# Gate one-hots made on POOL, and more gathered rows worked off in the u loop of a PEER layer

## The reference, cut to what matters

```python
def peer_ffn(h, w_query, sub_keys, u_tab, v_tab):
    q = (h @ w_query).reshape(bsz, seq, 8, 2, 128)
    scores = einsum('blhcd,hckd->blhck', q, sub_keys)      # 128 keys per half
    s_top, i_top = top_k(scores, 16)
    cand_s = s_top[..., 0, :, None] + s_top[..., 1, None, :]      # 16 x 16 pairs
    best_s, pos = top_k(cand_s, 16)
    expert_idx = i_top[0] * 128 + i_top[1]                 # at pos: one of 16384
    gates = softmax(best_s)
    act = gelu(einsum('td,thkd->thk', h_blk, u_tab[expert_idx]))
    out = einsum('thkd,thk->td', v_tab[expert_idx], gates * act)
```

## Time and profile before

| | |
|---|---|
| median of three runs | 3818.42 us |
| profiled execution, its own time | 3818.46 us |
| its span | 3816.6 us |
| busy: PE, DVE, ACT, POOL | 3387.5, 2730.8, 1932.5, 607.7 us |
| expert stage, a block | 36.3 us |
| u loop | from 2544 to 3233 us of the span |
| v loop | from 3233 to 3808 us |

### The profile page before, as it was taken

The page is one execution under the profiler, slowest core; times in us unless marked ns, Lnnn a source line. Parts: engine busy times, 40 slices in busy tenths (PEclk is TensorE's granted clock), DMA queues, the critical chain, the costliest instruction groups (busy, mean ns, idle before and its releaser), DMA issues. The chain is left out here.

```text
span 3816.6 us, 46791 instructions
## 1 busy us (share of the span) xinstructions
PE 3387.5 (89%) x16253; PEld 2821.9 (74%) x16253; DVE 2730.8 (72%) x3557; ACT 1932.5 (51%) x2328; POOL 607.7 (16%) x428
## 2 busy tenths in 40 slices
PE   7697745999999999999299977799999987999998
PEld 3485544777777777777188856589999987777776
DVE  8316536999999999999544226337888766788887
ACT  1225414777777777777124334225878874332332
POOL 0000011001011011010200000000000254555652
PEclk9898867999999999999589978899999998999999
DMA  7520107999999999999633301134545689999997
GB/s 296 176 67 2 46 30 260 375 379 374 378 375 374 378 375 373 379 374 363 239 97 92 98 22 45 63 139 160 183 177 216 258 331 363 358 371 379 385 381 274
DMA packets 217467, 954.88 MB, mean 250 GB/s; under 512 B 23344, under 2 KB 85040, under 8 KB 142448
## 3 DMA queue, kind: packets, MB, share of 16 engines
q1 hardware_dynamic: 161872, 734.91, 52.0%
q0 software_dynamic: 46816, 167.80, 11.7%
q10 hardware_dynamic: 8640, 50.34, 3.2%
HBM read 864.92 MB, written 88.05 MB: 250 GB/s over the span
## 5 line engine op out<-in xcount | busy, mean ns | idle before, releaser
L1394 DVE TENSOR_TENSOR w_low<-w_raw,w_high 128x2048 fp32r<-128x2048 f32 x399 | 908.6, 2288 | 91.3 <-ACT w_high L1323 86.4
L1323 ACT ACTIVATE w_high<-w_raw 128x2048 fp32r<-128x2048 f32 x399 | 765.0, 1917 | 329.9 <-PE ps L125 182.3
L123 PE MATMUL ps<-w_high,xT_high 128*128 128x512 f32 x1056 | 433.6, 411 | 21.8 <-issue 21.8
L2462 DVE TENSOR_TENSOR uv_lo<-uv_raw,uv_hi 128x2048 fp32r<-128x2048 f32 x128 | 293.3, 2292 | 198.8 <-ACT uv_hi L2267 198.0
L124 PE MATMUL ps<-w_low,xT_high 128*128 128x512 f32 x1056 | 418.4, 396 | 0.0
L125 PE MATMUL ps<-w_high,xT_low 128*128 128x512 f32 x1056 | 418.1, 396 | 0.0
L123 PE MATMUL ps<-h4T_high,uv_hi 128*128 128x384 f32 x1024 | 355.9, 348 | 18.5 <-ACT a_out L2304 14.9
L123 PE MATMUL ps<-uv_hi,w_hi 128*128 128x512 f32 x768 | 306.3, 399 | 45.7 <-DVE w_lo L2477 34.8
L124 PE MATMUL ps<-h4T_low,uv_hi 128*128 128x384 f32 x1024 | 346.5, 338 | 0.0
L125 PE MATMUL ps<-h4T_high,uv_lo 128*128 128x384 f32 x1024 | 346.4, 338 | 0.0
L2267 ACT ACTIVATE uv_hi<-uv_raw 128x2048 fp32r<-128x2048 f32 x128 | 244.7, 1912 | 149.0 <-PE ps L125 119.2
(11 more groups left out here) (515 smaller groups left out, 6991.0 us busy)
## 6 DMA issues: line engine op xcount, KB each, us to landing
w_raw<-in_w_gate_up SPq DMA_DIRECT2D x267, 1024.0 KB, 6.9
w_raw<-in_w_down SPq DMA_DIRECT2D x132, 1024.0 KB, 6.9
uv_raw<-in_peer_u SPq DMA_DIRECT2D x64, 1024.0 KB, 5.3
uv_raw<-in_peer_v SPq DMA_DIRECT2D x64, 1024.0 KB, 9.3
wbuf_ada<-in_w_ada SPq DMA_DIRECT2D x12, 2048.0 KB, 8.8
a_rows<-a_out SPq DMA_DIRECT2D x128, 192.0 KB, 2.0
g_rows<-spread ACTq DMA_DIRECT2D x12, 2048.0 KB, 8.4
qT<-g_rows SPq DMA_DIRECT2D x16, 1536.0 KB, 15.1
```

The lines of the kernel that those rows point to most:

```text
L123: pe.matmul(out, l_hi, r_hi, start=first, stop=False)
L1323: act.activation(w_hi[:, n % SPLIT, :], w_raw[:, n % RAW, :], ACT.Copy).then_inc(s_wh, 1)
L1394: dve.tensor_tensor(w_lo[:, n % SPLIT, :], w_raw[:, n % RAW, :], w_hi[:, n % SPLIT, :].bitcast(F32), ALU.subtract).then_inc(s_wl, 1)
L2462: dve.tensor_tensor(uv_lo[:, n % 2, :], uv_raw[:, n % 2, :], uv_hi[:, n % 2, :].bitcast(F32), ALU.subtract).then_inc(s_lo, 1)
```

## The change

- Both hots of every token are made on POOL, one instruction each: tensor_scalar with is_equal against the index, and for first_hot a multiplication with the gate in the same instruction. That is 8 instructions a round, 768 in all. POOL's program becomes a walk over the plan: in each step the hots, then the gathers that the plan lets go in this step (`gather_step`).
- `gated_hots` on ACT and `one_hots` on DVE go. selT keeps three parts of five, for the negated copies are not needed; PE waits for one semaphore in place of two.
- ORDER is (1, 0, 2, 3) and SPARSE 1: tile 0 is selected second, in steps 12 to 22 rather than 24 to 34. Rows start in step 24: one a step to 33, mostly two to 45, six in 46 to 59, four to 63, two a step in the v loop. 137 of the 256 are then done in the u loop.
- The rounds go 1, 1, 2, ... in steps 11 to 33 and 2, 3, 2, ... in steps 34 to 59. MIDDLE_AT (from which row on four more homes are used) goes from 8 to 43, LATE_AT (the tenth home) from 84 to 140.
- In the expert stage a tile room_xT of 432 floats a partition, which nothing uses, is allocated ahead of xT_high.

```diff
     xe = sb(stage, "xe", [P, D])
+    sb(stage, "room_xT", [P, 432])
     xT_hi, xT_lo = (sb(stage, f"xT_{x}", [P, 2, 4 * P], F32R) for x in ("high", "low"))
...
-    ORDER, SPARSE = (1, 2, 0, 3), 2
+    ORDER, SPARSE = (1, 0, 2, 3), 1
-    selT = sb(peer, "selT", [P, 2, 5, P])
+    selT = sb(peer, "selT", [P, 2, 3, P])
-    MIDDLE_AT, LATE_AT = 8, 84
+    MIDDLE_AT, LATE_AT = 43, 140
-    hots_in = [[1] + [2] * 15 + [1], [2, 2, 2, 1] * 4 + [2, 2], [2, 3] * 6 + [2]]
-    hots_from = (11, 28, 46)
-    rows_in = {45: 2, 46: 4} | {n: 4 for n in range(47, NG)} | {NG + k: 3 if k % 9 else 2 for k in range(NG - 1)}
+    hots_in = [[1, 1, 2] * 4 + [1, 1, 1, 2] * 2 + [2, 2, 2], [2, 3] * 6 + [2], [2, 3] * 6 + [2]]
+    hots_from = (11, 34, 47)
+    rows_in = {n: 1 for n in range(24, 34)} | {n: 2 for n in range(34, 47)} | {n: 6 for n in range(47, 60)} | {n: 4 for n in range(60, NG)}
+    rows_in |= {34: 5, 46: 6}
+    rows_in |= {NG + k: 2 if k % 3 == 0 else 2 for k in range(NG - 1)}
...
+            def hots(r):
+                s, tile = r % HOTS, 4 * r // P
+                if r * 4 % P == 0:
+                    pool.wait_ge(s_selh, tile + 1)
+                if r >= HOTS:
+                    pool.wait_ge(s_gb, r - HOTS + 1)
+                at = 4 * r % P
+                for q in range(4):
+                    pool.tensor_scalar(first_hot[:, s, q, :], iota_row[:, :], selT[:, tile % 2, 0, at + q:at + q + 1],
+                                       selT[:, tile % 2, 2, at + q:at + q + 1], ALU.is_equal, ALU.mult).then_inc(s_hotp, 1)
+                    pool.tensor_scalar(second_hot[:, s, q, :], iota_row[:, :], selT[:, tile % 2, 1, at + q:at + q + 1], None,
+                                       ALU.is_equal).then_inc(s_hotp, 1)
...
+            for n in range(2 * NG):
+                for kind, x, c in plan[n]:
+                    if kind == "H":
+                        for k in range(c):
+                            hots(x + k)
+                for g in gathers_at[n]:
+                    gather(g)
...
             def gate_products(r):
-                pe.wait_ge(s_hot, 2 * (r + 1))
-                pe.wait_ge(s_hota, 3 * (r + 1))
+                pe.wait_ge(s_hotp, 8 * (r + 1))
```

More of the change, by code:

```diff
@@ L2058, in emit @@
         sem(f"peer_{x}") for x in ("scores", "scores_read", "shifted", "exp", "selected", "sel_turned", "sel_here"))
-    s_hi, s_lo, s_used, s_pa, s_gelu, s_hot, s_dist, s_hota, s_gb, s_gt2, s_gst = (
-        sem(f"peer_{x}") for x in ("high", "low", "split_used", "dots", "gelu", "one_hots", "distances", "gated_hots", "gate_products",
+    s_hi, s_lo, s_used, s_pa, s_gelu, s_hotp, s_gb, s_gt2, s_gst = (
+        sem(f"peer_{x}") for x in ("high", "low", "split_used", "dots", "gelu", "one_hots", "gate_products",
                                    "gates_spread", "gates_stored"))
@@ L2083, in emit @@
     UNITS_T, UNIT_EXP = 21, 14
-    turns_at = {x: [at + k for k in range(11)] for x, at in enumerate((0, 12, 24, 35))}
-    hots_in = [[1] + [2] * 15 + [1], [2, 2, 2, 1] * 4 + [2, 2], [2, 3] * 6 + [2]]
-    hots_from = (11, 28, 46)
-    rows_in = {45: 2, 46: 4} | {n: 4 for n in range(47, NG)} | {NG + k: 3 if k % 9 else 2 for k in range(NG - 1)}
+    turns_at = {x: [at + k for k in range(11)] for x, at in enumerate((0, 12, 23, 35))}
+    hots_in = [[1, 1, 2] * 4 + [1, 1, 1, 2] * 2 + [2, 2, 2], [2, 3] * 6 + [2], [2, 3] * 6 + [2]]
[3 more added lines that the diff above has]
+    rows_in |= {NG + k: 2 if k % 3 == 0 else 2 for k in range(NG - 1)}
     plan, count, at = [[] for _ in range(2 * NG)], [0] * TT, 0
@@ L2104, in emit @@
     assert left == 0
+    work_step = [n for n in range(2 * NG) for kind, x, c in plan[n] if kind == "S" for _ in range(c)]
+    first_step = max(turns_at[SPARSE]) + 1
+    gather_step = [work_step[before_of[g]] if before_of[g] >= 0 else first_step for g in range(2 * SEL)]
+    for g in range(2 * SEL):
+        if g >= MIDDLE_AT:
+            gather_step[g] = max(gather_step[g], max(turns_at[TT - 1]) + 1)
+        gather_step[g] = max(gather_step[g], gather_step[g - 1] if g else 0)
+        assert gather_step[g] <= work_step[g]
     exp_at, sel_at, scores_at, count = {}, {}, {}, [0] * TT
@@ L2118, in emit @@
     places = [((), (3,), (2, 6), (1, 4, 7))[len(rounds)] for rounds in rounds_in]
+    gathers_at = [[g for g in range(2 * SEL) if gather_step[g] == n] for n in range(2 * NG)]
     turned_before = [sum(y != SPARSE for y in range(x)) for x in range(TT + 1)]
@@ L2126, in _, with gather @@
         def _(pool):
[L2127 to L2131, removed]
+            def hots(r):
[10 more added lines that the diff above has]
+                                       ALU.is_equal).then_inc(s_hotp, 1)
+            def gather(g):
+                if g == 0:
+                    pool.wait_ge(s_xr, 16)
+                    pool.wait_ge(s_sel, SPARSE + 1)
                 if g == MIDDLE_AT:
@@ L2141, in _ @@
                                         bass.IndirectOffsetOnAxis(ap=row_id[:, k:k + 1], axis=0)).then_inc(s_row[home_of[g]], 16)
+            u_table = t["peer_u_rows"]
+            v_table = t["peer_v_2"].rearrange("k n (j d) -> (k n j) d", d=D)
+            for n in range(2 * NG):
[5 more added lines that the diff above has]
+                    gather(g)
         @block.sync
@@ L2282, in spread_round @@
                     act.dma_start(g_rows[h, :, :], spread_flat).then_inc(s_gst, 16)
[L2284 to L2298, removed]
             def gelu(m):
@@ L2308, in take_selected @@
                 if tile >= 2:
-                    act.wait_ge(s_hot, 2 * (tile - 1) * P // 4)
+                    act.wait_ge(s_hotp, 8 * (tile - 1) * P // 4)
                 src = ps[:, 2, 0:3 * P].rearrange("p (c n) -> p c n", c=3)
-                act.activation(selT[:, tile % 2, 0:3, :], src, ACT.Copy)
-                act.activation(selT[:, tile % 2, 3:5, :], src[:, 0:3:2, :], ACT.Copy, scale=-1.0).then_inc(s_selh, 1)
+                act.activation(selT[:, tile % 2, :, :], src, ACT.Copy).then_inc(s_selh, 1)
             high(0)
@@ L2319, in _ @@
                     rounds, early = rounds_in[n], sum(at < 4 for at in places[n])
-                    coming = list(rounds_in[n + 1]) if n + 1 < NG else []
-                    if coming and n not in sel_at:
-                        gated_hots(coming.pop(0))
                     for r in rounds[0:early]:
@@ L2327, in _ @@
                         take_selected(turned_before[sel_at[n]])
-                    for r in coming:
-                        gated_hots(r)
                     for r in rounds[early:]:
@@ L2429, in select @@
                 yield
[L2431 to L2442, removed]
             def row_work(g):
@@ L2488, in _ @@
                             next(tiles[x])
-                        elif kind == "H":
-                            one_hots(x + k)
-                        else:
+                        elif kind == "S":
                             rows.append(x + k)
@@ L2494, in _ @@
                     weights(n + 1 - NG)
-                    row_work(rows.pop(0))
+                    for g in rows[:1]:
+                        row_work(g)
                     weights_low(n + 1 - NG)
-                for g in rows:
+                for g in rows[1 if n >= NG else 0:]:
                     row_work(g)
```

## The result

The changed kernel takes 4104.77 us (median of 4 runs, 4103.17 to 4105.76); the kernel before took 3816.57 in its 4 runs. The ratio is 1.075 [1.073, 1.077]: 7.5% slower, where 3771 us, 1.2% faster, was forecast, and outside the range. The profiled execution took 4105.76 us, its span 4103.9.

The account below looks back on a forecast made before the run. PE bounds the expert stage and the u loop without gathers; steps 47 to 59 and the v loop exceed PE's need, with DMA waits. 3818.5 - 29 + 21 - 40 + 0 = 3770.5, forecast 3771 us, range 3735 to 3825.

Parts of the forecast that it names:

- POOL's price of a hot: Hots on POOL in the u loop: 0.38 us each including waits, bounds 0.29 and 0.48.
- the port rival: U loop: hots and DVE instructions wait for each other, 0.6 us a hot, +78 and +50, 3878 us; chance 0.12.
- The port: SBUF access in hot steps: POOL's hots and DVE instructions with two SBUF inputs take turns, so price above 0.29 us.
- The idle tile: Expert stage: operands a multiple of 512 B apart save 6.9 ns a matmul; -29 us, bounds 0 and -33.
- The v loop: Two gathered rows a step, not three, turn it from DMA to PE; -40 us, bounds -54 and -15.
- ACT's and DVE's relief: U loop: ACT's relief and DVE's load from the moved hots and added rows, taken together as 0.
- the part of DMA in steps 47 to 59: U loop: with hots of 0.29 us, DMA asks as much as POOL; the steps take 170 us, +4.
- +21 us in steps 47 to 59: U loop: POOL's hots and gathers set the pace at 15.0 us a step; 187 us in place of 166.
- 0.12 for slower: Whole kernel: the chance given to a slower result; faster had 0.78 and same 0.10.

Follow-up runs that it names:

- plan_alone: The changed kernel with the hots made on ACT and DVE as in the kernel before, not on POOL; 3772.62 us, ratio 0.9871 to the kernel before.

## Why the prediction was wrong

**The step that failed is POOL's price of a hot.** The prediction put it at 0.38 us including waits and bounded it by 0.29 and 0.48. It measured 0.69 by itself and 0.956 with the waits for DVE. The floor came from a select and the ceiling from the slope of a copy, "128 more columns are worth some 110 ns", with an allowance for a second pass and the scalars. No row of the trace had a tensor_scalar on POOL, and a plain comparison of 128 columns without any scalar read is already 531 ns, above that ceiling. The bounds were no bounds: both rows were of other operations. The Trainium skill's page "GPSIMD Engine Reference", section "Engine selection", calls GpSimd's elementwise work with one input roughly line-rate. For one of 128 columns the runs show another ratio: the same first_hot takes 342 ns on DVE and 788 on POOL. What more columns would cost was not tried, so nothing here tells a slow rate from a fixed cost.

**The sum would have shown the sign.** The prediction said that the port rival decides from 0.48 us a hot on; no run has a price near that threshold, so it is neither shown nor refuted. With 0.956 in its own formulas, steps 47 to 59 take 13 x (20 x 0.956 + 7.4) - 8 = 337 us, +171; steps 34 to 46 take 20 x 0.956 + 2.5 = 21.6 us each where PE wants 10.5, +144; with -29 and -40 that makes 4064 us. Measured were +189 and +129. The rest lies where the prediction had no term: +18 in steps 11 to 33, where PE's waits for POOL begin in step 27 (20.7 us in six waits), and +31 in steps 60 to 63. Of these, 20 are step 60, whose products use the hots of step 59, with PE waiting 15.2 us for POOL. The other 11 are step 63, which takes 30.8 us, but 30.3 in plan_alone too, so they come with the plan and not with the hots.

**The port.** The prediction saw it, named the rows of DVE as what the hots would meet, and gave it 12 in 100 at 0.6 us. It is real, but the smaller part: 205 us of the 734 that the hots take. Without it 0.69 us alone would have been over 0.48. That the two engines take turns, as the prediction put it, holds for the hots that meet DVE, and hardly for DVE.

**The idle tile** was sized right: -29 forecast, -28 measured, the spacing and the cause as reasoned.

**The v loop** was put at -40 with bounds of -54 and -15, and gave -51. The guess that the reads of the gates would still delay reads of activations was too careful; with two rows a step every step but the first takes 8.2 or 8.3 us.

**ACT's and DVE's relief at 0, and the plan.** What the relief is worth in the changed kernel can't be read, because POOL sets its pace. plan_alone shows the plan without it: 3772.6 us. By stretches its u loop is 10 us shorter than before in steps 11 to 33, then 24, 8 and 11 us longer (34 to 46, 47 to 59, 60 to 63), 33 in all, and the v loop is 50 shorter. The prediction had +4 for the part of DMA in steps 47 to 59; it is 173.9 - 166.0 = 8.

**The forecast's total** of 3771 us equals that of plan_alone, which is the change without the part whose price was wrong. The agreement is a coincidence: the forecast has +21 us in steps 47 to 59 and 0 elsewhere in the u loop, and plan_alone has the four terms just named. The chances failed with it: 0.12 for slower rested on the same ceiling.

## What to carry to other kernels

Before work is moved to an engine, look for a row of that very operation on that engine; where there is none, a row of another operation gives no upper bound, and the forecast should ask at which price the sign turns and give the side beyond it real weight. An engine that looks idle may have no time to spare for work that stands in one queue with gathers and feeds the engine that sets the pace: count its queue step by step, and count on a price that rises with what the work meets on the other engine. In a loop bound by PE look at the distance between the operands as well: 320 bytes off a multiple of 512 cost 3% here, and 48 idle floats took it away.

## What the runs showed of the hardware that was not expected

- A matmul of 512 columns takes 226.8 ns when its two SBUF operands start a multiple of 512 bytes apart, and 233.1 to 233.6 ns when they are 320 bytes off it; moving both together changes nothing. Other distances were not tried.
- POOL's tensor_scalar on 128 x 128 float32 takes 531 ns with one operation and a constant, 591 with a scalar from SBUF, 647 with two operations and constants, and 788 with two scalars from SBUF, with a spread of a few ns.
- A POOL instruction that meets DVE instructions with two SBUF inputs can wait for more than one in a row, up to 4.9 us for 0.79, while DVE's row products in x_sb grow by 4% (1218 to 1267 ns). A DVE instruction that begins while a hot is running takes 0.08 us longer on the mean of 56 cases.
